# Windowed attention with its banded key blocks divided into 64 by 64 quadrants

## What is computed

```python
# 8 query heads, 2 key/value heads, head width 64, blocks of 128 tokens
kw, vw = band(k), band(v)                 # for each block: previous, own and next key block
s_loc = einsum('bnqhgd,bnjhd->bnhgqj', qb, kw) * scale
s_ctx = einsum('bnqhgd,bchd->bnhgqc', qb, kc) * scale       # 256 context keys, all open
rel = kj - BLOCK - qi                                       # key position - query position
valid = (abs(rel) <= 128) & (kpos >= 0) & (kpos < L)
s_loc = where(valid, s_loc, NEG_INF)
probs = softmax(concatenate([sink, s_ctx, s_loc]))
out = probs[ctx] @ vc + probs[loc] @ vw
```

## Time and profile before

| what | us |
|---|---|
| median of 3 runs (982.45, 984.50, 1005.12) | 984.5 |
| the profiled execution | 986.05 |
| span of its slowest core (core 2) | 984.4 |
| spans of the eight cores | 975.5 to 984.4 |
| TensorE busy on core 2 | 889.6 |
| ScalarE, VectorE busy | 285.5, 482.3 |

### The profile page before, as it was taken

One profiled execution on the slowest core, in us unless ns is written; L12 is line 12 of the kernel. 1 busy time (PEld: TensorE's weight loads), 2 busy tenths in 40 slices (PEclk: granted clock), 3 DMA queues, 4 the chain that ended last, 5 costly groups with the idle time before them and its releaser, 6 DMA issues.

```text
span 984.4 us, 15135 instructions; the slowest of 8 cores (975.5 to 984.4 us)
## 1 busy us (share of the span) xinstructions
PE 889.6 (90%) x5195; PEld 427.0 (43%) x5273; DVE 482.3 (49%) x946; ACT 285.5 (29%) x392; POOL 239.2 (24%) x282
## 2 busy tenths in 40 slices
PE   0568898889989999999998999999999999999993
PEld 0324444545544444444443444444444444444442
DVE  2147564466742366567677411122211114777774
ACT  1225545489932223332332311111111110000000
POOL 5024333266632345445443103010000000000000
PEclk9999898999999999999999999999999999999997
DMA  8999785159730023236845139962211004333231
GB/s 168 172 198 207 151 189 75 23 97 180 146 119 1 1 97 108 65 98 151 170 128 107 44 65 156 169 102 43 43 17 27 1 1 150 105 110 122 93 107 45
DMA packets 57964, 99.68 MB, mean 101 GB/s; under 512 B 20896, under 2 KB 21408, under 8 KB 57888
## 3 DMA queue, kind: packets, MB, share of 16 engines
q0 software_dynamic: 21136, 40.44, 26.4%
q1 hardware_dynamic: 36752, 58.25, 19.5%
HBM read 118.14 MB, written 16.78 MB: 137 GB/s over the span
## 4 chain that ended last, share of the span: by engine, by line
PE 71%; DMA 9%; DVE 6%; ACT 6%; issue 4%; POOL 1%; SPq 0%; another core or an unknown queue 0%; DVEq 0%; ACTq 0%; POOLq 0%
PE bank L1073 27%; PE bank L953 15%; PE bank L1204 14%; DMA arena<-wada 7%; ACT arena L812 4%; PE bank L984 4%; PE bank L488 2%; DMA arena<-xh 2%; PE bank L809 1%; PE bank L558 1%; PE bank L528 1%; DVE arena L1028 1%; PE bank L805 1%; PE bank L828 1%; DVE arena L1044 1%
## 5 line engine op out<-in xcount | busy, mean ns | idle before, releaser
L1073 PE MATMUL bank<-arena 128*128 128x512 bf16 x1380 | 303.8, 379 | 4.4 <-DVE arena L1084 1.9
L1073 PEld LDWEIGHTS bank<-arena 128*128 128x128 bf16 x1408 | 137.6, 98 | 169.7 <-issue 4.6
L953 PE MATMUL bank<-arena 128*128 128x512 bf16 x752 | 166.9, 379 | 2.2 <-DVE arena L969 0.9
L1084 DVE TENSOR_TENSOR arena<-bank,arena 128x512 bf16<-128x512 f32 x88 | 60.8, 692 | 217.6 <-PE bank L1073 209.5
L1204 PE MATMUL bank<-arena 128*128 128x512 bf16 (+1 forms) x734 | 151.5, 366 | 0.7
L1082 ACT ACTIVATE arena<-bank 128x512 f32<-128x512 f32 x88 | 52.2, 595 | 219.1 <-PE bank L1073 219.0
L953 PEld LDWEIGHTS bank<-arena 128*128 128x128 bf16 x768 | 74.9, 98 | 92.3 <-issue 2.7
L1204 PEld LDWEIGHTS bank<-arena 128*128 128x128 bf16 x748 | 73.2, 98 | 79.1
L969 DVE TENSOR_TENSOR arena<-bank,arena 128x512 f32<-128x512 f32 x64 | 43.2, 690 | 84.1 <-PE bank L953 65.5
L812 ACT ACTIVATE arena<-bank 128x1024 bf16<-128x1024 f32 x80 | 76.3, 1027 | 4.8 <-PE bank L809 4.5
L962 ACT ACTIVATE arena<-bank 128x512 f32<-128x512 f32 x64 | 36.7, 591 | 101.9 <-PE bank L953 101.9
(11 more groups left out here) (107 smaller groups left out, 869.6 us busy)
## 6 DMA issues: line engine op xcount, KB each, us to landing
arena<-xh SPq DMA_DIRECT2D x34, 512.0 KB, 6.1
arena<-wada POOLq DMA_DIRECT2D x12, 1024.0 KB, 17.2
arena<-wff POOLq DMA_DIRECT2D x11, 1024.0 KB, 10.0
xmid_d<-arena SPq DMA_DIRECT2D x16, 512.0 KB, 2.9
arena<-xmid_d SPq DMA_DIRECT2D x16, 512.0 KB, 3.8
out<-arena SPq DMA_DIRECT2D x32, 256.0 KB, 2.0
arena<-wff POOLq DMA_DIRECT2D x11, 512.0 KB, 20.0
arena<-wout SPq DMA_DIRECT2D x16, 256.0 KB, 4.5
```

What stands on the lines that cost most here:

```text
L953: t_mm = S.op('pe', lambda e, k=k, n=n, p=bk(bank), lhs=w[:, lo + k, :], rhs=src[:, k, tok]: e.matmul(p, lhsT=lhs, rhs=rhs, start=(k == 0) ...
L1073: rhs=h2T[:, k, tok]: e.matmul(p, lhsT=lhs, rhs=rhs, start=(k == 0), stop=(k == 7)),
L1084: fb_free[b0 + 1] = sg_free[s_] = t_act[(f, tg)] = S.op('dve', lambda e, f=f, p=bk(b0 + 1), sg=sgb[s_]: e.tensor_tensor(out=act[f][:, tok] ...
```

## The change

The five key blocks per tile become four and a half. Chunk 0 ("a") holds the previous block's 128 keys for queries 0 to 63 and the next block's 128 keys for queries 64 to 127: 1024 columns, masked after exp on VectorE as before (`att_mask`, issued later in the iteration). Chunk 2 ("b") holds the two remaining quadrants that are not closed: on partitions 64 to 127 the previous block's keys 64 to 127 for queries 64 to 127, on partitions 0 to 63 the next block's keys 0 to 63 for queries 0 to 63: 512 columns, the mask added by two identity matmuls of 256 columns. The two closed quadrants are gone, and so is half an exp.

- Scores: chunk 0 is four matmuls of form 64*128 and 256 columns, chunk 2 four of form 64*64 and 256 columns.
- Value matmuls: seven per head in place of five: own block (128*128), two of form 128*64 for chunk a (output partitions 0 to 63, then 64 to 127), two of form 64*64 for chunk b, two context blocks (128*128). 56 per tile in place of 40.
- The first value matmul of a head waits for all five exps of its tile.
- Loop: head 7 of tile j-1 and `att_norm(j-1, 1)` move into iteration j behind scores 0; chunk a has three buffers. Per iteration: scores 0, head 7 of j-1, gmlp, scores 1, heads 0 and 1, mask and scores 2, head 2, transposes of j-1, scores 3, head 3, scores 4, heads 4 to 6.
- `att_mask(0)` is issued right ahead of the loop, behind the last projections.
- The mask input grows from 4 x 128 to 5 x 128 columns.

```diff
     def att_scores(j, s):
...
+        n_ = 512 if s == 2 else 1024
+        q0, kp, kn = j * 128, colpos(j), colpos(j + 2)
...
+        if s == 2:
+            v = 0 if j == 0 else 2 if j == NT - 1 else 1
             for kv in range(2):
+                S.op('pe', lambda e, psb=bk(2 * i2 + kv)[:, 0:256], mb=masks[:, 3 + v // 2:4 + v // 2, (v % 2) * 64:(v % 2 + 1) * 64]: e.matmul(
+                    psb, lhsT=ident, rhs=mb.to_broadcast([128, 4, 64]), start=True, stop=False), deps=deps if kv == 0 else (), sig=False)
+            parts = [(bk(2 * i2 + kv)[(1 - h) * 64:(2 - h) * 64, 0:256], kT, kv,
+                      (kp + 64, kn)[h], 64, (q0 + 64, q0)[h], 64) for h, kv in ((0, 0), (1, 1), (1, 0), (0, 1))]
+        elif s == 0:
+            parts = [(bk(2 * i2 + kv).rearrange('p (a b) -> p a b', a=4)[:, :, h * 64:(h + 1) * 64], kT, kv,
+                      (kp, kn)[h], 128, q0 + h * 64, 64) for h in range(2) for kv in range(2)]
+        else:
+            parts = [(bk(2 * i2 + kv), kT if s == 1 else kcT, kv, k0, 128, q0, 128) for kv in range(2)]
...
+    def att_mask(j):
...
     def att_pv(j, kv, gs):
...
+            mms = [(o_, ps_[:, c], vs[:, kv, 0:65]), (o_[0:64], pa[:, cl], vp[:, kv, 0:65]), (o_[64:128], pa[:, cr], vx[:, kv, 0:65]),
+                   (o_[0:64], pb[0:64, cb], vx[0:64, kv, 0:65]), (o_[64:128], pb[64:128, cb], vp[64:128, kv, 0:65]),
+                   (o_, p3[:, c], vcaug[:, 0, kv, 0:65]), (o_, p4[:, c], vcaug[:, 1, kv, 0:65])]
+            for i, (dst, p, v) in enumerate(mms):
+                t_mm = S.op('pe', lambda e, dst=dst, p=p, v=v, i=i: e.matmul(dst, lhsT=p, rhs=v, start=(i == 0), stop=(i == 6)),
+                            deps=[[att[j]['p'][n] for n in range(5)], o_free[kv], t_v[j:j + 3], t_vc] if i == 0 else (),
+                            sig=(g == 3 and i == 6))
...
+    att_mask(0)
     for j in range(NT + 1):
-        nxt = j + 1 < NT
-        cur = j < NT
+        prv, cur, nxt = j > 0, j < NT, j + 1 < NT
         if nxt:
             att_scores(j + 1, 0)
+        if prv:
+            att_pv(j - 1, 1, (3,))
+            att_norm(j - 1, 1)
         if cur:
             gmlp_tile(j)
...
         if nxt:
             att_scores(j + 1, 2)
+            att_mask(j + 1)
         if cur:
-            att_pv(j, 0, (2, 3))
-        if cur:
-            att_norm(j, 0)
-        if 0 <= j - 1:
+            att_pv(j, 0, (2,))
+        if prv:
             att_turn(j - 1)
         if nxt:
             att_scores(j + 1, 3)
         if cur:
-            att_pv(j, 1, (0, 1))
+            att_pv(j, 0, (3,))
+            att_norm(j, 0)
         if nxt:
             att_scores(j + 1, 4)
         if cur:
-            att_pv(j, 1, (2, 3))
-            att_norm(j, 1)
+            att_pv(j, 1, (0, 1, 2))
             wout_step(j)
```

More of the change, by code:

```diff
@@ L164, in build_nc @@
     ropes_d = din("ropes", [128, TH])
-    masks_d = din("masks", [128, 4 * 128])
+    masks_d = din("masks", [128, 5 * 128])
     ident_d = din("ident", [128, 128])
@@ L193, in build_nc @@
     perm, _, _ = A.alloc(BF16, [128])
-    masks, _, _ = A.alloc(BF16, [4, 128])
+    masks, _, _ = A.alloc(BF16, [5, 128])
     esink, _, _ = A.alloc(F32, [8])
@@ L778, in gmlp_out @@
         sbt_free[r] = t_yb[t]
-    pt_free = [None] * NPT
+    pt_free = {}
     yatm_free = [None, None]
@@ L785, in build_nc, with key_dep @@
     att = [dict(p={}) for _ in range(NT)]
[L787 to L795, removed]
+    def key_dep(kt):
+        return t_kg[4 if kt in (0, NT + 1) else (kt - 1) // 4]
@@ L797, in att_scores, with pt_buf @@
+    def pt_buf(j, s):
+        if s == 0:
+            return ('a', j % 3), flat(PT[(0, 5, 7)[j % 3]])
+        if s == 2:
+            return ('b', j % 2), flat(PT[2])[:, (j % 2) * 512:(j % 2 + 1) * 512]
+        return (s, j % 2), flat(PT[(j % 2) * 5 + s])
     def att_scores(j, s):
-        slot = (j % 2) * 5 + s
-        ksrc, _, _, t_k = att_srcs(j)[s]
+        key, pt = pt_buf(j, s)
         i2 = sc_st['i'] % 2; sc_st['i'] += 1
-        masked = s == 2
-        if masked:
-            mi = 3 if j == NT - 1 else 2
-            for kv in range(2):
-                S.op('pe', lambda e, psb=bk(2 * i2 + kv), mi=mi: e.matmul(
-                    psb, lhsT=ident, rhs=masks[:, mi:mi + 1, :].to_broadcast([128, 4, 128]), start=True, stop=False),
-                    deps=[s_free[i2], T_CONST] if kv == 0 else (), sig=False)
@@ L808, in att_scores @@
[L808 to L819, removed]
+        n_ = 512 if s == 2 else 1024
+        q0, kp, kn = j * 128, colpos(j), colpos(j + 2)
+        if s in (0, 2):
+            deps = [s_free[i2], key_dep(j), key_dep(j + 2), t_qg[j // 4], T_CONST]
+        else:
+            k0, t_k = (colpos(j + 1), key_dep(j + 1)) if s == 1 else ((s - 3) * 128, t_kc)
+            deps = [s_free[i2], t_k, t_qg[j // 4]]
@@ new lines, in att_scores @@
+        for n, (dst, src, kv, k_, kl, q_, ql) in enumerate(parts):
+            t_mm = S.op('pe', lambda e, dst=dst, src=src, kv=kv, k_=k_, kl=kl, q_=q_, ql=ql, first=(s != 2): e.matmul(
+                dst, lhsT=src[kv * 64:(kv + 1) * 64, k_:k_ + kl], rhs=qT[kv * 64:(kv + 1) * 64, :, q_:q_ + ql],
+                start=first, stop=True), deps=deps if n == 0 else (), sig=(n == len(parts) - 1))
+        s_free[i2] = att[j]['p'][s] = S.op('act', lambda e, pt=pt, psb=bk2(2 * i2), n_=n_: e.activation(
+            out=pt.rearrange('p (a b) -> p a b', a=2),
+            in_=psb.rearrange('p (a b) -> p a b', a=2)[:, :, 0:n_ // 2], func=AF.Exp, scale=0.125),
+            deps=[t_mm, pt_free.get(key)])
@@ L821, in att_pv @@
+    def att_mask(j):
+        v = 0 if j == 0 else 2 if j == NT - 1 else 1
+        att[j]['p'][0] = S.op('dve', lambda e, pt=pt_buf(j, 0)[1].rearrange('p (a b) -> p a b', a=8), v=v: e.tensor_tensor(
+            out=pt, in0=pt, in1=masks[:, v:v + 1, :].to_broadcast([128, 8, 128]), op=ALU.mult), deps=[att[j]['p'][0], T_CONST])
     def att_pv(j, kv, gs):
-        base = (j % 2) * 5
-        srcs = att_srcs(j)
         ob = bk(4 + kv).rearrange('p (a b) -> p a b', a=4)
-        order = (1, 0, 2, 3, 4)
+        vp, vs, vx = vaug[:, j], vaug[:, j + 1], vaug[:, j + 2]
+        pa, ps_, pb, p3, p4 = [pt_buf(j, n)[1] for n in range(5)]
@@ L826, in att_pv @@
         for g in gs:
[L827 to L830, removed]
+            h = kv * 4 + g
+            o_ = ob[:, g, 0:65]
+            c, cl, cr = slice(h * 128, (h + 1) * 128), slice(h * 128, h * 128 + 64), slice(h * 128 + 64, (h + 1) * 128)
@@ L833, in att_pv @@
             if kv == 1:
-                for s in range(5):
-                    pt_free[base + s] = t_mm
+                for n in range(5):
+                    pt_free[pt_buf(j, n)[0]] = t_mm
     def att_norm(j, kv):
@@ L1363, in prep_inputs @@
     off = np.float32(-2.0 ** 20)
-    full = np.full((128, 128), off, np.float32)
-    maskN = (1.0 - maskN) * off
-    zero = np.zeros((128, 128), np.float32)
     bc = lambda v: np.ascontiguousarray(np.broadcast_to(v[None, :], (128, v.shape[0])))
@@ L1383, in prep_inputs @@
         rc, rs = _rope_tables(start)
-        mk = np.stack([zero if seg == 0 else maskP, maskP, maskN, full if seg == 3 else maskN], 1).reshape(128, 512)
+        edges = [(seg > 0, True), (True, True), (True, seg < 3)]
+        mk = np.zeros((128, 5, 128), np.float32)
+        for n, (p, q) in enumerate(edges):
+            mk[:, n, :64] = maskP[:, :64] * p
+            mk[:, n, 64:] = maskN[:, 64:] * q
+            mb = mk[:, 3 + n // 2, (n % 2) * 64:(n % 2 + 1) * 64]
+            mb[:64] = (1.0 - maskN[:64, :64] * q) * off
+            mb[64:] = (1.0 - maskP[64:, 64:] * p) * off
+        mk = mk.reshape(128, 640)
         m = dict(shared)
```

3 lines of the change are left out of this document (added).

## The result

The changed kernel took 1061.2 us as median of 4 runs; against the kernel before the ratio is 1.0762 (95% interval 1.0696 to 1.0829). It is slower by some 75 us, more than twice the 33 that were forecast, inside the range, and within 2 us of the first rival's price (1063). One of the four runs took 1197.5 us, with the cores of one die at a mean clock of 0.79, and is left out of the ratio.

A forecast was written before the change was run, and what follows sets the result against it. ScalarE looked full before; after the change TensorE sets 6.88 us a tile: (6.88 - 4.97) x 15 = 28.7, end 3.1, start 1.0, together 32.8 us on 986.05, 1018.9 profiled, 1017 as median; range 1000 to 1064.

The forecast's parts named there:

- first rival: Attention stage: the clock falls to 1.2 GHz, 9.7 us a tile, 1063 us if at once on the slowest core; chance 0.34.
- the new stage is never idle, only short of columns: Attention stage: the argument against a fall of the clock there, which was priced at 77 us with the ends.
- full clock: Attention stage: the forecast's own case, changes of form at full clock, period 6.88 us, 1017 us; chance 0.50.
- Three changes of form a head at 0.10 us: Value matmuls on TensorE: three changes of form per head where there was none; 0.505 us a head, where five took 0.15.
- two-change rival: Value matmuls: no change of form between 128*64 and 64*64, period 5.9 us, 1002 us as median; chance 0.12.
- Quadrant matmuls side by side: Value matmuls of form 64*64: the two run side by side; between 0 and 0.03 us a head, taken as 0.
- Mask of the first tile: Start of the attention loop: tile 0's value matmuls begin 0.7 to 1.3 us later, behind `att_mask(0)`; +1.0 us.
- Fewer exps would thus shorten the stage: Attention stage: ScalarE looks full, so half an exp less saves 0.67 us per tile if ScalarE stays the bound.
- last rival: Attention stage: changes of form are free for half tiles, each tile gains 0.67 us, 976 us; chance 0.03.
- The saving stays: Attention stage: TensorE needs 4.2 us, under ScalarE's 4.3, so each tile gains 0.67 us, 976 us; chance 0.03.

The follow-up runs named there:

- first run with repeats: The changed kernel with the scores matmuls of chunks 1, 3 and 4 issued twice, 1536 more columns per tile; median 1087.6 us, lowest of 4 1074.6 us.
- runs with repeats: The changed kernel with scores matmuls issued repeatedly, 1536 useless columns per tile in one run, 2560 in the other; medians 1087.6 and 1031.4 us.
- woven kernel: The changed kernel with value matmuls of four heads placed next to other work of their form, 7 to 8 changes of form per tile, not 35; ratio 1.0074.

## Why the prediction was wrong

**The number.** The step that failed is the weighing of the first rival: "the new stage is never idle, only short of columns" was set against a fall of the clock, and the forecast given to the full clock with 0.50 against 0.34. The clock fell on all cores, and the forecast's sum had this term at nothing. The price of the fall had been worked out right: a period of 9.7 us against 9.83 measured, 1063 against 1061.2. The prediction had noted that the end of the stage on cores 0 and 5, behind which the clock fell, streamed about as thin as the new stage would; it set that aside because that end has gaps and the new stage has none. The first run with repeats shows that this argument doesn't hold: the clock fell on core 1 after 37 us without a gap. The measured time lies in the range only because the range was drawn to hold this rival too.

In the profiled executions, from the loop's first gmlp to C1, the stage took 153.5 us on core 1 after and 78.8 on core 2 before, 74.7 more. At full clock 15 iterations cost (6.82 - 4.97) x 15 = 27.7 (forecast 28.7), and what follows the last gmlp is 3.4 longer (8.1 in place of 4.7), some low clock in it. The other 43.6 is the clock, 1.6 less than 15 times its price of 3.01 a tile, since the first iteration was partly at the high level and the last shorter.

**Point by point.**
- Three changes of form a head at 0.10 us, 64*64 among them: right. At full clock a head between two scores takes 0.60 us (0.505 and 0.095 were forecast), by the rows of the first run with repeats, core 1. The two-change rival is out; it needed a period of 5.9, and the runs with repeats give 6.82.

```profile
219.60 0.67 PE L852 MATMUL bank<-arena 128*128 128x65 bf16 x7
220.20 0.61 PE L826 MATMUL bank<-arena 64*128 64x512 bf16 x4
```

- Quadrant matmuls side by side though they share a bank: right, by the same sum.
- Mask of the first tile: forecast +1.0 before the value matmuls. They began 1.08 us after scores 1 (200.54 to 201.62 on core 1), where before it was 0.49 (201.44 to 201.93 on core 2): +0.6.
- "Fewer exps would thus shorten the stage": wrong, and of no weight for the number, since TensorE set the pace anyway. The 0.67 us a tile of the last rival wasn't ScalarE's to give: half an exp alone gave nothing, because beside the exps, with the pause of 0.24 us in the earlier trace rows, runs a TensorE chain as long as they are.
- The saving stays: out for this order. With the forms woven the period went to 4.48 (forecast 4.3), so 0.49 of the 0.67.

## What to carry to other kernels

Before matmuls are cut into half tiles, count the changes of form that their order makes, and price each at what the trace shows between its present forms: sorting the same matmuls by form took a tile from 6.8 to 5.7 us, weaving them among other work of their form to 4.5. Where a stage gets longer without streaming more columns, read the clock as a term of its own: it can cost more than the edit (44 against 28 us here), it comes per core, and useless columns that hold it can pay. And a pause of an otherwise full engine may be the end of another chain: follow it before halving that engine's work.

## What the runs showed of the hardware

- In a stage that streams thinly the fall tends to stay: on core 0 of the first run with repeats, at 0.50 from about 194 us until C1 was under way (368), the same program ran as on core 1, which kept 1.00 until 238. So the same work kept the high level on one core and for 174 us didn't bring it back on another; of the six cores that had lost it early, only core 3 got it back within the stage, for 17 us. In the woven kernel the falls within the stage lasted 3.4 us each. The Trainium skill, TensorE: Matmul & The Clock Gate (section HAM oscillation — how this bites in real kernels), warns of idle gaps; on this core 1 TensorE had none in the 37 us before, and its clock fell all the same.
- A change of form costs nearly the same at either level: one head with its four changes took 0.60 us at 1.00 (219.60 to 220.20 in the rows above) and 0.77 at 0.50 (247.23 to 248.00 in the changed kernel's order of time, below), and its 325 streamed columns alone are 0.14 of the 0.17.

```profile
247.23 0.85 PE L850 MATMUL bank<-arena 128*128 128x65 bf16 x7
248.00 0.64 PE L761 MATMUL bank<-arena 128*64 128x128 bf16 x8
```

- The Trainium skill, TensorEngine Tiling (Array Packing), Key Properties, has it that a change of tiling mode drains the engine; these runs agree, for 64*64 too, at about 0.1 us each.
- Short dense matmuls beside heavy loads can stop TensorE for up to 2.9 us in the middle of a group; it goes on each time 1.2 to 1.6 us after a 16 KB load of the instruction queue has landed. Between 205 and 262 us, on all cores together, there were 30 such stops with 16 weight loads in 11 tiles, 22 with 16 in 16, 11 with 8 in 16, and none without. In the kernel before, where these instruction loads are 9 to 10 us apart on average and not 7 to 8, the steady iterations are 4.97 us but for one or two of 5.01 to 5.07 on each core.
